# Merges, output projection and up projection of a hybrid layer: splits issued one stage earlier, single-pass loops written out

## The chip, the cores and the metric

The kernel runs on one core of a Trainium2 chip. The metric is device time in microseconds (us). TensorE (PE) multiplies, VectorE (DVE) and ScalarE (ACT) do the elementwise work, SyncE (SP) issues most loads, GpSimd (POOL) a few stores. Every engine runs its own instructions in the order written; engines meet only at semaphores.

## The reference, cut to what matters

Two transformer blocks, sequence 512, width 1024, everything in float32. The change touches the end of the first block:

```
oa = gated delta rule (8 heads);  ob = retention (4 heads)       # before the change's stages
ya = oa @ w_br_a;  yb = ob @ w_br_b                               # 2048 -> 1024 each
mix = (sigmoid(gate_a) * ya + sigmoid(gate_b) * yb) @ w_out       # the gates are 1024 columns each of xn @ w_in
x = x + rmsnorm(mix, norm_mix_post)
hn = rmsnorm(x, norm_mlp_pre)
ff = square(relu(hn @ w_up)) @ w_down                             # 1024 -> 4096 -> 1024
x = x + rmsnorm(ff, norm_mlp_post)
```

The second block (neighbourhood, grouped and memory attention, 16 experts) follows and is not touched.

## The kernel before, in words

A float32 product is made of three passes. Each operand is split in two parts: ACT writes the high part (`high`, L81 to L83), DVE the low part as operand minus high part (`low`, L86 to L88), and PE multiplies low by high, high by high, high by low (`product`, L91 to L96). So each weight piece of 128 x 1024 words costs one `high` on ACT, one `low` on DVE and 24 matmuls of 512 columns on PE. The high parts lie in a ring of four (`hq`), the weights in three slots (`ring_b`, the same memory as `ring`), loaded by SP, 2 MB each; a low part overwrites its weight in place. The activations are transposed, `AT` (low) and `at_hi` (high), 4 row tiles of 128 beside one another.

The stages around the change, in the order in which PE runs them:

- End of head 3 of the retention: PE `scores_b`, `values_b` (fp32 matmuls), ACT the row norms (`attn_b`), DVE `gate_b` (L2353), PE `turn_b` (16 transposes, L1643), DVE `out_b` (L2361).
- Four merges: (x, c) = (0,0), (0,1), (1,0), (1,1), with x the branch and c the half of the columns. Each has 4 gates (24 matmuls each), then 4 blocks b of the branch product (48 matmuls each): 288 matmuls of 512 columns. It needs 12 weight pieces w0 to w11: w0 to w3 for the gates, w4 to w11 for the branch. For c = 0 the branch output `oT` (16 blocks) is loaded from DRAM (`load_o`, L491) and split too, 8 `high` and 8 `low`. The result goes to `mixT` (DVE L2404, or L2406 and L2407).
- Output projection (`tail_major`, L1695): 8 weight pieces and 4 pieces of `mixT` are split; steps n = 0 to 3 run over all four row tiles, then per tile n = 4 to 7. A step (n, t) is 6 matmuls. Between, each tile is normalised twice and turned (`turn_o`, 8 transposes a tile, L1726).
- Up projection (`mlp_up`): 32 groups g of 24 matmuls, relu by DVE (L2498), square by ACT (L1140).
- Down projection: two halves of 16 steps of 24 matmuls, which split the weights and `ffT`.

Each of the later halves (merge c = 1, up projection i = 1) is written as a hardware loop that runs once: `with pe.Fori(1, 2) as c: merge(0, c)`. In the order written, each engine finishes one stage before it begins the next stage's splits: DVE's and ACT's `merge` begins with split w0, after the last product of the merge before; `mixT` is split after the last merge (`act.wait_ge(*m_vec[1]("mix3", 1))`, L1095); the pieces of the second up loop and of the down projection likewise. SP loads `oT` for x = 0 after `b_vec("oT3.3")` and the store `o.3` (L495, L496).

Of the kernel before, what the change touches and what calls it, by code (L numbers as in the profile page):

```python
# [6 lines left out]
ALU = mybir.AluOpType  # L7
# [91 lines left out]
def build(nc, T, out):  # L99
    with ExitStack() as ctx:  # L100
# [85 lines left out]
        (mix_hi,), _ = carve(work, 8192, [(KB, 512)])  # L186
        (ff_hi, ff_lo), _ = carve(work, 0, [(4, 2, 512), (4, 2, 512)])
# [219 lines left out]
        final_banks = (0, 1, 2, 6, 7, 3, 4, 5)  # L407
        l_ring = [ring[1], ring[0]]
# [12 lines left out]
        def only(i):  # L421
            return isinstance(i, int) and i == 0
# [5 lines left out]
        def _(sp):  # L428
# [52 lines left out]
            def load_merge(x, c, before=None):  # L481
# [3 lines left out]
                srcs = (W[:, :, bass.ds(c * 512 + col, 512)], wb[0][:, :, bass.ds(c * 512, 512)], wb[1][:, :, bass.ds(c * 512, 512)])  # L485
                for q in range(3):
                    sp.wait_ge(*(before[q] if before else m_pe[x](("gate3", "lo3", "y3")[q], c - 1)))
                    m_w[x][q].start()
                    m_w[x][q].mark(sp.dma_start(ring_b[q], srcs[q]), "w")
# [4 lines left out]
            load_merge(0, 0, [bg_pe(f"g{g}.3") for g in (3, 7, 11)])  # L494
            sp.wait_ge(*b_vec("oT3.3"))  # L495
            sp.wait_ge(*ob_st_s("o.3"))  # L496
            load_o(0)
            with sp.Fori(1, 2) as c:
                load_merge(0, c)
            load_merge(1, 0, [m_pe[0](n, 1) for n in ("gate3", "lo3", "y3")])  # L500
            load_o(1)
            with sp.Fori(1, 2) as c:
                load_merge(1, c)

            WO = T["w_out"].rearrange("(k p) n -> p k n", p=P)
            for q in range(2):
                sp.wait_ge(*m_pe[1](("gate3", "lo3")[q], 1))
                o_w[q].mark(sp.dma_start(ring_b[q], WO[:, :, q * 512:(q + 1) * 512]), "w")
            sp.wait_ge(*m_vec[1]("mix3", 1))
# [6 lines left out]
            def load_up(i, before=None):  # L516
                for q in range(4):
                    sp.wait_ge(*(u_pe(f"g{4 * q - 5}", i) if q >= 2 else before[q] if before else u_pe(f"g{4 * q + 11}", i - 1)))
                    u_w[q].start()
                    u_w[q].mark(sp.dma_start(ring[q % 2], WU[:, :, bass.ds(i * 2048 + q * 512, 512)]), "w")  # L520
            load_up(0, [m_pe[1]("y3", 1), o_pe("m31")])
            with sp.Fori(1, 2) as i:
                load_up(i)

            def load_down(c):
                for q in range(4):
                    if q >= 2:
                        sp.wait_ge(*d_pe(f"p{4 * q - 5}.{c}"))
                    else:
                        sp.wait_ge(*(d_pe(("p11.0", "m3.0")[q]) if c else u_pe(f"g{4 * q + 11}", 1)))  # L530
                    d_w[q].mark(sp.dma_start(ring[q % 2], WD[q][:, :, c * 512:(c + 1) * 512]), f"w.{c}")
# [274 lines left out]
        def _(act):  # L806
# [228 lines left out]
            attn_b(B_HEADS - 1)  # L1035

            def merge(x, c):


                m_act[x].start()  # L1040
                first = only(c) and c == 0
                for n in range(12):
                    b = n - 4
                    if n % 4 == 0 and n < 8:
                        act.wait_ge(*m_w[x][n // 4]("w", c))
                    if n == 5:
                        act.wait_ge(*m_w[x][2]("w", c))
                    if n < 4:
                        if first and n == 0:
                            act.wait_ge(*(bg_pe("g11.3") if x == 0 else m_pe[0]("y3", 1)))  # L1050
                        elif not first:
                            act.wait_ge(*m_pe[x](("lo2", "y2", "lo3", "y3")[n], c - 1))
                    elif n < 8:
                        act.wait_ge(*m_pe[x](f"gate{b}", c))
                        if not first:
                            act.wait_ge(*m_vec[x](f"mix{b}", c - 1))
                        elif x == 1:
                            act.wait_ge(*m_vec[0](f"mix{b}", 1))
                        elif b == 0:
                            act.wait_ge(*b_vec("PT3.3"))  # L1060
                        m_act[x].mark(act.activation(sg[:, b, :], psum[b % 2][:, :], ACT.Sigmoid), f"sg{b}")
                    else:
                        act.wait_ge(*m_pe[x](("lo0", "y0", "lo1", "y1")[n - 8], c))
                    slot, q = (0, n) if n < 4 else (1 + n % 2, b // 2)
                    high(act, m_act[x], h_col[n % 4], ring_b[slot][:, :, q * P:(q + 1) * P], f"w{n}")
                    if n == 7 and first:
                        act.wait_ge(*ot_ld[x]("o"))
                        for k in range(8):
                            high(act, ot_act[x], oT_hi[:, 2 * k:2 * k + 2, :], oT[:, 2 * k:2 * k + 2, :], f"o{k}")
            merge(0, 0)  # L1070
            with act.Fori(1, 2) as c:
                merge(0, c)
            merge(1, 0)
            with act.Fori(1, 2) as c:
                merge(1, c)
# [19 lines left out]
            act.wait_ge(*m_vec[1]("mix3", 1))  # L1095
            for n in range(8):
                if n % 2 == 0:
                    high(act, o_act, mix_hi[:, n:n + 2, :], mixT[:, n:n + 2, :], f"mix{n // 2}")
                if n < 2:
                    act.wait_ge(*o_w[n]("w"))  # L1100
                if n >= 4:
                    act.wait_ge(*o_pe(f"p{n - 4}"))
                high(act, o_act, h_row[n % 4], ring_b[n % 2][:, n // 2 * 2:n // 2 * 2 + 2, :], f"w{n}")
            def norm_o(t):
                post_norm(o_act, o_vec, lambda t, c: 2 * t + c, lambda t, c: o_pe(f"m{t}{c}"), True, o_hN, t)

            def up_first(n):
                act.wait_ge(*o_pe(("r4", "r5", "m30")[n]))
                high(act, u_act, h_col[n], ring[0][:, :, n * P:(n + 1) * P], f"w{n}")
            u_act.start()  # L1110
            for t in range(3):
                norm_o(t)
            act.wait_ge(*u_w[0]("w"))
            up_first(0)
            split_tile(o_act, o_vec("AT01"), 0)
            norm_o(3)
            split_tile(o_act, o_vec("AT11"), 1)
            split_tile(o_act, o_vec("AT21"), 2)
            up_first(1)
            split_tile(o_act, o_vec("AT31"), 3)  # L1120
            up_first(2)

            def mlp_up(i):
                if not only(i):
                    u_act.start()
                for g in range(0 if only(i) else -3, 16):
                    n = g + 3
                    if n < 16:
                        if n % 4 == 0:
                            act.wait_ge(*u_w[n // 4]("w", i))  # L1130
                        if n >= 4:
                            act.wait_ge(*u_pe(f"g{n - 4}", i))
                        elif not only(i):
                            act.wait_ge(*u_pe(f"g{n + 12}", i - 1))
                        high(act, u_act, h_col[n % 4], ring[n // 4 % 2][:, :, n % 4 * P:(n % 4 + 1) * P], f"w{n}")
                    if g < 0:
                        continue
                    act.wait_ge(*u_vec(f"relu{g}", i))
                    at = bass.ds(i * 16 + g, 1)
                    u_act.mark(act.activation(ffT[:, at, :], ffT[:, at, :], ACT.Square), f"ff{g}")  # L1140
                    if only(i) and 9 <= g < 13:
                        q = g - 9
                        act.wait_ge(*p_vec(f"memT{q}"))
                        high(act, p_act, mem_hi[:, 2 * q:2 * q + 2, :], memT[:, 2 * q:2 * q + 2, :], f"mh{q}")
            mlp_up(0)
            with act.Fori(1, 2) as i:
                mlp_up(i)

            def mlp_down(c):
                for n in range(16):  # L1150
                    if n % 4 == 0:
                        act.wait_ge(*d_w[n // 4](f"w.{c}"))
# [264 lines left out]
        def _(pe):  # L1417
# [270 lines left out]
            with pe.Fori(1, 2) as c:  # L1688
                merge(0, c)
# [1227 lines left out]
```

## Time and profile before

| | us |
|---|---|
| median of 3 runs (2643.02 to 2647.59) | 2643.35 |
| the profiled execution, its own time | 2646.1 |
| its span, first to last instruction | 2644.3 |
| PE busy | 2454.5 (93%) |
| DVE busy | 1111.4 (42%) |
| ACT busy | 834.2 (32%) |
| mean granted TensorE clock, 1.0 is full | 0.970 |

The span and the run's own time differ by 1.8 us, which lies around the instructions. A matmul's duration in a row (0.39 us for 512 columns) includes its pipeline; how fast PE gets on is read from the starts. "[5.36 <-DVE work L2353]" at the end of a row says that the engine was idle 5.36 us before it, and who ended that.

### The profile page before, as it was taken

Reading aid. Unit: us, or ns where it says so; the run is one execution under the profiler, and the core shown is the slowest. Engines: PE = TensorE matmul, PEld = TensorE weight load, DVE = VectorE, ACT = ScalarE, POOL = GpSimd, SP = SyncE. Lnnn points to the kernel's source line nnn. Section 1 sums busy time; section 2 is a strip of 40 time slices with the busy share of each in tenths; the row PEclk is TensorE's granted clock in tenths of the full one; section 3 lists DMA queues with packets and bytes.
Section 4 is the critical chain, followed back from the end, with each engine's and each line's share of the span. In section 5 each row is a group of like instructions: output and inputs, shape, how many; then the busy total and the mean of one; then the engine's idle time right before and its main releaser. Section 6 shows DMA issues by size and latency. Waiting matters only on the chain.

```text
span 2644.3 us, 31184 instructions
## 1 busy us (share of the span) xinstructions
PE 2454.5 (93%) x13320; PEld 1833.8 (69%) x13320; DVE 1111.4 (42%) x1503; ACT 834.2 (32%) x1311; POOL 174.4 (7%) x159
## 2 busy tenths in 40 slices
PE   7999999999998999987999999978899969999997
PEld 5787888877776777776787887855678844454442
DVE  5747566343433323245334454457543441111223
ACT  6444534232322313133224343435522221110101
POOL 0202021111110000000000001121000000000000
PEclk9999999999998999998999999989999989999998
DMA  4112203132223223231222233231222369999995
GB/s 156 64 49 81 96 33 120 65 112 84 100 71 143 103 77 123 96 129 68 82 96 96 96 134 117 90 108 64 80 96 80 145 249 394 428 428 427 427 428 223
DMA packets 116665, 400.43 MB, mean 151 GB/s; under 512 B 6320, under 2 KB 24240, under 8 KB 103600
## 3 DMA queue, kind: packets, MB, share of 16 engines
q1 hardware_dynamic: 112368, 383.76, 37.9%
q0 software_dynamic: 4160, 14.68, 1.6%
q8 instruction: 106, 1.74, 0.3%
q14 instruction: 31, 0.25, 0.0%
HBM read 384.53 MB, written 13.89 MB: 151 GB/s over the span
## 4 chain that ended last, share of the span: by engine, by line
PE 83%; DVE 9%; ACT 4%; issue 2%; DMA 1%; SPq 0%; DVEq 0%; ACTq 0%
PE banks L94 19%; PE banks L96 19%; PE banks L95 19%; PE banks L2060 8%; PE banks L2089 4%; PE banks L2017 2%; DVE ring_split L88 1%; PE banks L1636 1%; PE banks L1534 1%; ACT halves_split L83 1%; DVE work L2791 1%; DMA work<-v_rows 1%; PE banks L1540 1%; DVE const L2585 1%; PE banks L1626 1%
## 5 line engine op out<-in xcount | busy, mean ns | idle before, releaser
L94 PE MATMUL banks<-work_split,ring_split 128*128 128x512 f32 x1536 | 624.7, 407 | 33.0 <-DVE ring_split L88 16.0
L88 DVE TENSOR_TENSOR ring_split<-ring,halves_split 128x1024 fp32r<-128x1024 f32 x284 | 355.8, 1267 | 673.0 <-ACT halves_split L83 672.9
L95 PE MATMUL banks<-work_split,halves_split 128*128 128x512 f32 x1536 | 605.9, 394 | 0.0
L96 PE MATMUL banks<-activations_T_split,halves_split 128*128 128x512 f32 x1184 | 467.6, 395 | 0.0
L83 ACT ACTIVATE halves_split<-ring 128x1024 fp32r<-128x1024 f32 x284 | 295.2, 1053 | 311.2 <-PE banks L96 255.9
L94 PEld LDWEIGHTS banks<-work_split,ring_split 128*128 128x128 f32 x1536 | 293.0, 191 | 106.1 <-issue 25.5
L95 PEld LDWEIGHTS banks<-work_split,halves_split 128*128 128x128 f32 x1536 | 293.6, 191 | 58.8 <-issue 1.0
L96 PE MATMUL banks<-ring_split,work_split 128*128 128x512 f32 (+1 forms) x736 | 285.2, 388 | 0.0
L95 PE MATMUL banks<-halves_split,work_split 128*128 128x512 f32 x672 | 263.9, 393 | 0.0
L96 PEld LDWEIGHTS banks<-activations_T_split,halves_split 128*128 128x128 f32 x1184 | 225.9, 191 | 48.9
L94 PE MATMUL banks<-halves_split,work_split 128*128 128x512 f32 x384 | 152.5, 397 | 10.1 <-DVE work_split L88 5.1
L96 PEld LDWEIGHTS banks<-ring_split,work_split 128*128 128x128 f32 x736 | 139.6, 190 | 28.5
L95 PEld LDWEIGHTS banks<-halves_split,work_split 128*128 128x128 f32 x672 | 127.7, 190 | 26.9 <-issue 0.7
L96 PE MATMUL banks<-work_split,halves_split 128*128 128x512 f32 x352 | 138.1, 392 | 0.0
L94 PE MATMUL banks<-halves_split,activations_T_split 128*128 128x512 f32 x288 | 116.5, 405 | 4.6 <-DVE ring_split L88 4.6
L2060 PE MATMUL banks<-ring,work 128*64 128x512 f32 x384 | 112.2, 592 | 5.6 <-DVE work L2791 5.2
L2060 PE MATMUL banks<-work 128*64 128x512 f32 x384 | 112.2, 593 | 4.2 <-DVE work L2791 4.2
L870 ACT ACTIVATE work<-banks 128x512 f32<-128x512 f32 x60 | 35.9, 598 | 192.4 <-PE banks L96 192.2
L1379 ACT ACTIVATE work<-banks 128x512 f32<-128x512 f32 x16 | 15.8, 1090 | 255.1 <-PE banks L2060 255.1
L2771 DVE TENSOR_TENSOR work<-banks,work 128x512 f32<-128x512 f32 x16 | 11.1, 692 | 202.2 <-ACT work L1379 202.2
L94 PEld LDWEIGHTS banks<-halves_split,work_split 128*128 128x128 f32 x384 | 73.4, 191 | 26.6 <-issue 5.9
L2060 PEld LDWEIGHTS banks<-ring,work 128*64 128x64 f32 x384 | 38.7, 137 | 71.2 <-issue 71.2
(339 smaller groups left out, 3186.4 us busy)
## 6 DMA issues: line engine op xcount, KB each, us to landing
ring<-w_in_in SPq DMA_DIRECT2D x31, 2048.0 KB, 7.8
work<-w_gate_up_in SPq DMA_DIRECT2D x24, 2048.0 KB, 18.2
ring<-w_gate_up_in SPq DMA_DIRECT2D x24, 2048.0 KB, 18.1
ring<-w_down_in SPq DMA_DIRECT2D x20, 2048.0 KB, 10.1
work<-w_down_in SPq DMA_DIRECT2D x9, 2048.0 KB, 14.9
ring<-w_in_in SPq DMA_DIRECT2D x17, 1024.0 KB, 7.7
ring<-w_up_in SPq DMA_DIRECT2D x8, 2048.0 KB, 7.8
halves<-w_gate_up_in SPq DMA_DIRECT2D x8, 2048.0 KB, 19.6
```

The lines of the kernel that those rows point to most:

```text
L83: s.mark(act.activation(R(dst), src, ACT.Copy), what)
L88: s.mark(dve.tensor_tensor(R(dst), src, R(hi).bitcast(F32), ALU.subtract), what)
L94: pe.matmul(out, R(ll), R(rh), start=start, stop=False)
L95: pe.matmul(out, R(lh), R(rh), start=False, stop=False)
L96: return pe.matmul(out, R(lh), R(rl), start=False, stop=stop)
L870: g_act.mark(act.activation(dst, src, func), f"e{i}")
L1534: mm = pe.matmul(bank_c[j][h, c], X[j][h, t, :], PP[j][h, t, :], start=True, stop=True)
L1540: mm = pe.matmul(bank_b[j][h, c], PP[j][h, t, :], X[j][h, t, :], start=True, stop=True)
L1626: mm = pe.matmul(psum[2 + m][:, m * P:], qkT[:, 2 + k, m * P:(m + 1) * P], qkT[:, k, m * P:], start=(k == 0), stop=(k == 1))
L2017: mm = pe.matmul(psum[b // 4][:, b % 4 * P:(b % 4 + 1) * P], XR[:, t, b * P:(b + 1) * P], SP[:, t, :], start=(t == 0), stop=(t == NT - 1))
L2060: mm = pe.matmul(psum[3 + c % 2 * 2 + c // 2][64 * e:64 * e + 64, :], xst[:, 2 * q + k, 64 * e:64 * e + 64], weights(12 * p + 2 * q + e, k ...
L2089: mm = pe.matmul(psum[4 + n][64 * e:64 * e + 64, :], actT[:, 4 * a + k, 64 * e:64 * e + 64], weights(12 * p + 8 + 2 * a + e, k * DM + n * ...
```

## The change

- The single-pass loops are written out; signal names carry the half (`w0.1`), addresses become constants. The number of instructions in the bodies stays.
- PE runs the first two gates of merge (0,0) between `values_b(3)` and `turn_b(3)`. ACT and DVE split w0 to w3 of it before `attn_b(3)` and `gate_b(3)`. DVE's `out_b(3)` moves behind w5. SP loads `oT` of x = 0 after `b_pe("O3.3")`, and the wait for store `o.3` moves to the load for x = 1.
- `oT` is split in groups of three beside the gates 1 to 3, no more after all of them.
- In each merge ACT splits w0 to w3 of the next one at its end; DVE splits w0 in front of product 2, w1 in front of product 3.
- `mixT`'s first two pieces are split in merge (1,1); `mix_hi` moves to `at_hi`'s memory. The order of the output projection's pieces becomes `o_order`, which uses the first column half's slot first. The first three up pieces are split between the output pieces 5 and 7, with buffers of their own (`up_hi`).
- The norms: the gain `norm_mix_post` is multiplied before the root is there, residual add and scale are one instruction, `norm_mlp_pre` is a row (`pre_row`, one more 512 KB load on SP in front of the memory tokens and the first up weights) multiplied in with the second norm, and the transposed tiles are split straight from PSUM in halves. ACT loads the Sqrt table ahead.
- `turn_o(1)` runs inside tile 3; the up projection begins with groups 0 to 2 on the columns 0 to 255 (row tiles 0 and 1), `turn_o(3)` behind group 0, then the columns 256 to 511.
- The first three weight pieces and two `ffT` pieces of the down projection are split in g = 28 to 30; `ffs` has 8 places.

The core of the diff:

```diff
             scores_b(B_HEADS - 1)
             values_b(B_HEADS - 1)
+            gate_m(0, 0, 0)
+            gate_m(0, 0, 1)
             turn_b(B_HEADS - 1)
...
-            with pe.Fori(1, 2) as c:
-                merge(0, c)
+            for m in range(4):
+                x, c = merge_of(m)
+                for b in range(2 if m == 0 else 0, 4):
+                    gate_m(x, c, b)
                 for b in range(4):
+                    branch_m(x, c, b)
...
-            sp.wait_ge(*b_vec("oT3.3"))
+            sp.wait_ge(*b_pe("O3.3"))
+            load_o(0)
+            load_merge(0, 1)
+            load_merge(1, 0)
             sp.wait_ge(*ob_st_s("o.3"))
-            load_o(0)
...
             x_back.mark(sp.dma_start(XR, T["x"].rearrange("(t p) d -> p t d", p=P)), "x")
             o_row.mark(sp.dma_start(row, T["norm_mix_post"].broadcast_to([P, DM])), "row")
+            o_row.mark(sp.dma_start(pre_row, T["norm_mlp_pre"].broadcast_to([P, DM])), "pre")
...
+            # ACT, one merge
+                for b in range(4):
+                    gate_m(x, c, b)
+                    split_m(x, c, b + 4)
+                    if c == 0 and b:
+                        if b == 1:
+                            act.wait_ge(*ot_ld[x]("o"))
+                        for k in range(3 * b - 3, min(3 * b, 8)):
+                            high(act, ot_act[x], oT_hi[:, 2 * k:2 * k + 2, :], oT[:, 2 * k:2 * k + 2, :], f"o{k}")
+                if (x, c) == (1, 1):
+                    high_mix(0)
+                    high_mix(1)
+                for n in range(8, 12):
+                    split_m(x, c, n)
+                if (x, c) != (1, 1):
+                    for n in range(4):
+                        split_m(nx, nc_, n)
...
+            # ACT, output projection
+            high_o(4)
+            high_o(5)
+            high_up(0)
+            high_up(1)
+            high_o(6)
+            high_up(2)
+            high_o(7)
+            act.activation(nmax[:, 0:1], eps, ACT.Sqrt)
...
+            # DVE, norms of the output projection
+            for t in range(2):
+                weighed_o(t)
+                post_o(t)
+                pre_o(t)
+            weighed_o(2)
+            post_o(2)
+            low_t(0)
+            pre_o(2)
+            weighed_o(3)
+            post_o(3)
+            low_t(1)
+            low_t(2)
+            pre_o(3)
+            low_t(3)
...
+            # PE
+            turn_o(2)
+            for t in range(2):
+                pe.wait_ge(*o_vec(f"ATl{t}1"))
+            for g in range(3):
+                pe.wait_ge(*u_vec(f"w{g}"))
+                up(g, 0, 256)
+                if g == 0:
+                    turn_o(3)
+            for t in range(2, 4):
+                pe.wait_ge(*o_vec(f"ATl{t}1"))
+            for g in range(32):
+                if g < 3:
+                    mm = up(g, 256, 512)
...
+                # ACT (DVE the same with low_), behind the square of group g
+                if 28 <= g < 31:
+                    high_down(g - 28, 0)
+                if 28 <= g < 30:
+                    high_ff(g - 28, 0)
```

## Rows read from the trace of the kernel before

**Rows 1.** The page: busy time of each engine, share of the span, instructions.
```profile
PE 2454.5 (93%) x13320; PEld 1833.8 (69%) x13320; DVE 1111.4 (42%) x1503; ACT 834.2 (32%) x1311; POOL 174.4 (7%) x159
```

**Rows 2.** Waits of PE, 834 to 1400 us: total, times, longest.
```profile
PE banks L94 <- DVE ring_split L88: 17.6, 6, 5.0
PE banks L94 <- DVE work_split L88: 13.3, 3, 5.1
PE banks L1726 <- DVE work L2433: 10.2, 2, 8.1
...
PE banks L94 <- DVE activations_T_split L88: 5.1, 1, 5.1
```

**Rows 3.** Stretches: length, busy (count) PE, PEld, DVE, ACT, POOL; PEclk, DMA, GB/s.
```profile
834.40:919.90 85.50, 74.03 (x305) 60.36 (x304) 31.23 (x32) 28.52 (x32) 0.75 (x1) 0.90 0.29 103
919.90:989.00 69.10, 67.20 (x288) 55.10 (x288) 16.93 (x16) 11.49 (x13) 0.00 (x0) 0.98 0.26 92
989.00:1064.40 75.40, 68.82 (x289) 56.16 (x288) 28.18 (x27) 25.10 (x27) 0.00 (x0) 0.95 0.38 139
1064.40:1134.00 69.60, 66.94 (x289) 54.99 (x288) 19.70 (x20) 11.49 (x13) 0.00 (x0) 0.98 0.26 92
1134.00:1206.60 72.60, 52.37 (x224) 42.91 (x224) 42.73 (x57) 32.47 (x53) 0.00 (x0) 0.83 0.32 118
1206.60:1389.90 183.30, 179.56 (x784) 148.02 (x784) 62.48 (x69) 49.16 (x64) 0.00 (x0) 0.98 0.23 81
1389.90:1401.10 11.20, 6.12 (x15) 4.86 (x16) 9.32 (x9) 8.32 (x9) 0.00 (x0) 0.70 0.51 189
```

**Rows 4.** Timeline of PE, 878.90 to 884.81: first and last of 27 starts.
```profile
878.90 0.39 PE L94 MATMUL banks<-work_split,ring_split 128*128 128x512 f32 x1
...
884.81 0.39 PE L96 MATMUL banks<-work_split,halves_split 128*128 128x512 f32 x1
```

**Rows 5.** Timeline of PE at the start of merge (0,0), and one turn at 1180.
```profile
839.83 3.67 PE L1643 MATMUL banks<-const,work 128*128 128x128 f32 x16 [5.36 <-DVE work L2353]
845.48 0.79 PE L94 MATMUL banks<-work_split,ring_split 128*128 128x512 f32 x1 [1.98 <-DVE ring_split L88]
...
1180.02 1.03 PE L1726 MATMUL banks<-const,work 128*128 128x128 f32 x8
```

**Rows 6.** Stretches: half-clock start, long dense stretch, 48 matmuls of 256 columns, a turn.
```profile
840.00:848.00 8.00, 6.03 (x22) 5.14 (x23) 6.71 (x8) 0.59 (x1) 0.75 (x1) 0.50 0.27 101
1402.00:1566.00 164.00, 164.00 (x725) 135.78 (x724) 71.81 (x66) 59.40 (x66) 0.00 (x0) 1.00 0.26 93
1577.60:1583.60 6.00, 6.00 (x51) 5.89 (x50) 6.00 (x8) 2.65 (x4) 0.00 (x0) 1.00 0.90 316
1180.00:1186.40 6.40, 6.40 (x34) 5.35 (x33) 4.19 (x8) 2.90 (x8) 0.00 (x0) 1.00 0.00 0
```

**Rows 7.** Timeline of DVE across a merge boundary; at 1139.75 ACT's splits.
```profile
919.92 0.69 DVE L2404 TENSOR_TENSOR work<-banks,residual 128x512 f32<-128x512 f32 x1 [10.19 <-PE banks L96]
920.53 4.62 DVE L88 TENSOR_TENSOR ring_split<-ring,halves_split 128x1024 fp32r<-128x1024 f32 x4
...
1139.75 1.99 ACT L83 ACTIVATE halves_split<-ring 128x1024 fp32r<-128x1024 f32 x2
```

**Rows 8.** DMA: size and time to landing, in the windows of their issue.
```profile
work<-o_a SPq DMA_DIRECT2D x1, 4096.0 KB, 13.7
work<-o_b SPq DMA_DIRECT2D x1, 4096.0 KB, 18.3
ring<-w_up_in SPq DMA_DIRECT2D x1, 2048.0 KB, 15.9
```

**Rows 9.** Timeline, last tile of the output projection, DVE and ACT.
```profile
1192.21 0.59 ACT L1081 ACTIVATE work<-banks 128x512 f32<-128x512 f32 x1
...
1195.09 1.23 DVE L2427 TENSOR_TENSOR residual<-residual,work 128x1024 f32<-128x1024 f32 x1
1196.34 1.06 ACT L1087 ACTIVATE work<-residual 128x1024 f32<-128x1024 f32 x1 [2.93 <-DVE residual L2427]
```

More of the change, by code:

```diff
@@ L514, in _, with load_up @@
             WD = T["w_down"].rearrange("(a k p) n -> a p k n", p=P, a=4)
[L516 to L523, printed above, removed]
+            def load_up(n):
+                if n >= 2:
+                    sp.wait_ge(*u_pe(f"g{4 * n - 5}"))
+                else:
+                    sp.wait_ge(*(m_pe[1]("y3.1"), o_pe("m31"))[n])
+                u_w[n % 4].mark(sp.dma_start(ring[n % 2], WU[:, :, n * 512:n * 512 + 512]), f"w{n // 4}")
+            for n in range(8):
+                load_up(n)
             def load_down(c):
@@ L1034, in _ @@
                 step_b(h)
-            attn_b(B_HEADS - 1)
[L1037 to L1069, printed above, removed]
@@ L1077, in post_norm, with high_mix @@
+            def high_mix(n):
+                act.wait_ge(*m_vec[1]("mix3.0" if n < 2 else f"mix{2 * n - 3}.1"))
+                high(act, o_act, mix_hi[:, 2 * n:2 * n + 2, :], mixT[:, 2 * n:2 * n + 2, :], f"mix{n}")
+            for n in range(4):
+                split_m(0, 0, n)
+            attn_b(B_HEADS - 1)
+            for m in range(4):
+                merge(*merge_of(m))
             def post_norm(act_s, vec_s, bank, last, prenorm, hN, t):
@@ L1104, in norm_o @@
[L1104 to L1144, printed above, removed]
@@ L1160, in mlp_down @@
[L1160 to L1161 removed]
+                    if c or n >= 3:
+                        high_down(n, c)
+                    if c or n >= 2:
+                        high_ff(n, c)
             for c in range(2):
@@ L1687, in _, with tail_major @@
-            merge(0, 0)
-            with pe.Fori(1, 2) as c:
-                merge(0, c)
-            merge(1, 0)
-            with pe.Fori(1, 2) as c:
-                merge(1, c)
-            def tail_major(vec_s, pe_s, hi, lo, view, rows, between, second=None):
+                    branch_m(x, c, b)
+            def tail_major(vec_s, pe_s, hi, lo, view, rows, order, between, second, inside=None):
                 def step(n, t):
-                    k, c = n // 2 * 2, n % 2
+                    k, c = order[n]
@@ L1704, in tail_major @@
                     pe.wait_ge(*vec_s(f"w{n}"))
-                    if n == 1 and second:
+                    if order[n] == (0, 1):
                         second()
@@ L1757, in _, with up @@
-            mlp_up(0)
-            with pe.Fori(1, 2) as i:
-                mlp_up(i)
+            pe.wait_ge(*m_act[1]("sg3.1"))
+            pe.wait_ge(*m_vec[1]("mix2.1"))
+            tail_major(o_vec, o_pe, mix_hi, mixT, ring_b, h_row, o_order, lambda t: turn_o(0) if t == 2 else None,
+                       lambda: pe.wait_ge(*m_vec[1]("mix3.1")), lambda t, n: turn_o(1) if (t, n) == (3, 5) else None)
+            turn_o(2)
+            def up(g, c0, c1):
+                for k in range(KB):
+                    mm = product(pe, psum[g % 4][:, c0:c1], (up_slot(g)[:, k, :], up_piece(g)[:, k, :]), (at_hi[:, k, c0:c1], AT[:, k, c0:c1]),
+                                 k == 0, k == KB - 1)
+                return mm
@@ L2415, in post_norm @@
+            decay_b(B_HEADS - 1)
+            for n in range(4):
+                split_m(0, 0, n)
+            gate_b(B_HEADS - 1)
+            for m in range(4):
+                merge(*merge_of(m))
             def post_norm(act_s, vec_s, bank, rowsig, pt_tmp, t):
```

475 lines of the change are left out of this document (279 added, 196 removed).

## The prediction

> **What bounds the kernel now.** The page comes first: PE is busy 93% of the span, DVE and ACT under half [rows 1]. So time can only be won where PE stands idle or runs at its lower clock, and the next view is the list of what PE waited for in the part that the change touches. Nearly every wait there ends with DVE, although DVE has time to spare: 17.6 us for low parts of weights, 13.3 for low parts of activations, 10.2 for a normalised tile, 5.1 for the last turned tile [rows 2], and 5.36 before the 16 transposes of head 3, which is the wait that the list's cut leaves out [rows 5]. Together 51.6 us. The reader is to see that these are not waits for a busy engine but for an order: at a merge boundary DVE writes the last product at 919.92 and only then, back to back, the low parts that the next gates need [rows 7].
>
> The third view is the table of stretches, for the idle time has a companion. Between two starts PE takes (884.81 - 878.90) / 26 = 0.227 us for a matmul of 512 columns [rows 4]. A merge has 288, which is 65.5 us; the stretches of the four merges are 85.5, 69.1, 75.4 and 69.6 [rows 3], more than 65.5 plus their waits. The rest is the clock: after 5.36 and 1.98 us of idleness the granted clock is 0.50, that is 1.2 of 2.4 GHz [rows 6], and each matmul issued then costs about 0.2 us more. A dense stretch of 164 us shows 1.00 throughout [rows 6]. So each wait is worth itself and one to three us behind it, and length minus counted work gives both at once; I use that.
>
> No loop overhead shows: the four low parts at 920.53 follow the product without a gap [rows 7], and each loop runs once. Writing the loops out is worth 0 by itself (below and above: 0.1 us a boundary, some 0.5 in all, from the gap at 919.92); what counts is the order that it allows.
>
> **Part by part.** Unit costs: a high part 1.0 us on ACT, a low part 4.62 / 4 = 1.15 on DVE, a 128x512 product from PSUM 0.69 [rows 7]; 8 transposes 1.03 with their pipeline, 0.85 to the next start, at full clock, 16 of them 3.67 at half clock [rows 5].
>
> (a) Merge (0,0). The stretch of 85.5 holds 65.5 of matmuls and 16 transposes, 1.7 at full clock: 18.3 lost. After: the two gates (48 x 0.227 = 10.9 us) run while ACT takes the row norms and DVE gates the head; DVE is done with that at 839.8, PE asks for it only at about 834.4 + 10.9 = 845.3. The load of `oT` is now issued at 834.5 instead of 849.4 and takes 13.7 [rows 8], landing at 848.2, while the first branch product comes at 834.4 + 65.5 / 3 + 1.7 = 857.9. In between DVE has four products for head 3 (4 x 0.81), the first three pieces of `oT` by 854.7, w6, three more by 859.3; PE needs piece k at 857.9 + 1.36 k. The last two, behind w7, are there at 863.0, needed at 866. Nothing late: gain 18.3. If the two gates did not start at once (w0 needs ACT and DVE before 834.4, both idle from 826), the loss would be 1 to 2.
>
> (b) Merge (0,1): 69.1 - 65.5 = 3.6 lost to w0, which now is split before product 2. Its slot is loaded when the gates end, 44 us earlier. Gain 3.6.
>
> (c) Merge (1,0): 75.4 - 65.5 = 9.9. w0 as in (b). `oT` of x = 1 takes 18.3 [rows 8] beside a weight load and is issued no earlier than before, 0.5 after the last product. Count from that product: landing 18.8, gates end 21.8. ACT makes o0 to o2 by 21.7, then the late sigmoid and w6, o3 to o5 by 26.2, w7, o6 and o7 by 29.7; DVE follows by about 1.2 to 1.8: o3 25.7, o5 28.0, o6 30.3, o7 31.5. PE wants them at 25.9, 28.6, 30.0, 31.3. About 0.4 late. Gain 9.5. A load 2 us later would make it 7.5.
>
> (d) Merge (1,1): 69.6 - 65.5 = 4.1, all of it w0. Gain 4.1. The two pieces of `mixT` that ACT and DVE take on in this merge lie in the 16 us between w7 and w8.
>
> (e) Output projection to the first up matmul: 72.6 us with 192 matmuls (43.6) and 32 transposes (3.4), 25.6 lost. Its start waits for nothing any more. Three new costs. First, the up weights: their load took 15.9 from 1136.91, so it landed 18.8 after the last product [rows 8, 3]; with one more 512 KB in front, at about 0.4 MB a us, 20.2. ACT, in order, stands at that load in front of output pieces 6 and 7: up0 21.3, up1 22.3, o6 23.3, up2, o7 25.2, and DVE has o6 at 24.9 and o7 at 27.2. PE wants them at 24.5 and 25.9: about 1.4 late. Second, the tail. Let M be the last output matmul. On the last tile the residual add began 2.88 after its second square [rows 9], of which about 1.4 were the two products by the root; now they stand in front of it, and of the second one (0.69) the root hides half. So the residual begins at M + 2.0 and, 1.23 long, ends at 3.25; then DVE takes the two halves of tile 1 (2 x 0.69), so PE may begin the up projection at M + 4.75 with tiles 0 and 1. `turn_o(2)` fills 0.85 of it; 3.9 idle. DVE goes on with tile 2 to 6.1 and ends `hn3` at M + 7.5; PE has used 3.0 for the half group and asks at 7.75. Tile 3's low halves are there at about 11.1; the half groups 1 and 2 end at 14.6. Third, the half groups: 48 matmuls of 256 columns took 6.0 us [rows 6], 0.125 each; 144 of them cost 18.0 instead of 72 x 0.227 = 16.3, so 1.7 more. Sum 7.0; gain 18.6. The slow matmuls at the start of the up projection stay (they are in (f)). Bounds: 20.2 if the weights are in time and DVE's order hides half of the idleness, 13 if the load crawls at `o_a`'s 0.3 MB a us (landing 22, 3.2 late) and the clock stays low over the half groups.
>
> (f) Up projection: 183.3 with 768 matmuls (174.6) and 16 transposes (1.7), 7.0 lost. 1.6 is the slow start, kept; 5.4 is the wait for piece 16 and its clock, and the pipeline of three pieces ahead now runs through. Gain 5.4.
>
> (g) Down projection: 11.2 us up to full clock for 14 matmuls (3.2): 8.0 lost. The load is issued when g27 ends, as before; w0 is there 7.9 later, 2.4 after g28. ACT has w0 and the first `ffT` piece 4.5 after g28, DVE 5.7, with 16.3 us until the down projection. Pieces 2 and 3 of `ffT` wait for the last group and have 10.9 us. Gain 8.0. What is queued behind the waiting split in g = 28 is relu29 on DVE, needed for bank 1 a whole group later.
>
> Sum: 18.3 + 3.6 + 9.5 + 4.1 + 18.6 + 5.4 + 8.0 = 67.5 us. The profiled execution took 2646.1 (span 2644.3, 1.8 around it), which gives 2578.6; it is 2.75 above the median of the runs, and from 2643.35 the time is 2575.9. I forecast 2576.
>
> The granted clock once more, because the change puts transposes between short groups of matmuls. One turn of 8 inside dense work ran at 0.1 us each with the clock at 1.00, and so did what followed [rows 5, 6]. The Trainium skill, "TensorE: Matmul & The Clock Gate", section "Part 4: PE-mode transpose", states that transposes don't count as PE work for the clock gate in the way matmuls do and don't bring its full rate. By that rule `turn_b` and the turns around the up projection's start would cool the engine; the trace can't refute it, as its one full-speed turn is short and lies in dense work.
>
> **The rivals.**
>
> R1, the clock falls at the turns. 16 transposes between gates would be 3.7 instead of 1.7 and 13 gate matmuls behind them 0.2 dearer (2.0 + 2.6, priced as after the turn at 839.83 [rows 5]); the half groups around `turn_o(3)` would take 0.21 for a matmul over two groups instead of 0.125 (48 x 0.085 = 4.1), less 1.6 counted already. Together 7: 2583. For it: the slow starts follow turns at 845 and 1206. Against it: real idleness stands before each of these.
>
> R2, the waits come back as new ones. ACT and DVE are queues, and a split that now stands in front of a needed product or sigmoid blocks it where its weights or its buffer come late; the up weights are the case that I can see, `oT` of (1,0) the next. If half of (b), (d), (f), (g) and of the tail remained, that is 0.5 x (3.6 + 4.1 + 5.4 + 8.0 + 12) = 16.5, it is 2592. Against it: in all of these the slack worked out is over 5 us.
>
> R3, slower than before. Denser work could make the chip grant less. It decides at a point: PE would have to spend 67.5 / 0.5 = 135 us of the 499 that remain of these 566.7 at 1.2 GHz, and at half of them it would be 2576 + 125 = 2701. Against it: 164 dense us at 1.00 [rows 6].
>
> R4, the change doesn't do what it says: the first product in each stage still finds its split behind another wait, since the order in DVE's queue and not PE's asks decides. Then only the work moved in (a) and (c) pays, some 25 us: 2618.
>
> **How the numbers follow.** The forecast holds with 0.62, R1 0.15, R2 0.15, R4 0.04, R3 0.03; 0.01 is for something without effect. The forecast's own range is 2571 to 2581 (the bounds of (c), (e)). To leave no more than 2 in 10 out, the range takes in R1 and most of R2: 2569 to 2591. What a measurement can tell from no change is 0.2%, 5 us: faster 0.95, same 0.01, slower 0.04.
>
> **What would show it.** In the changed kernel's rows: no wait of PE over 1 us from the end of `values_b` to the output projection's pieces 6 and 7, and the four merges 65 to 66 us each, the first with its transposes; about 1 us before each of those two pieces, on low parts of `ring`; one wait of some 4 us between `turn_o(2)` and the half group 0, with slow matmuls behind it; from there to the second half of the down projection none, where before 3.65 and 5.10 stood. The transposes of `turn_b` at 0.1 us refute R1, at 0.23 they bear it out. I am wrong in mechanism if the sum of PE's waits falls by about 45 us and the time doesn't follow by 60 or more: then something else, after this stage, gave the end.

## The result, and the profile after

The changed kernel takes 2576.41 us (median of 4 runs, 2572.77 to 2577.82) against 2643.86 for the kernel before in the same comparison; the ratio is 0.974, 95% interval 0.9728 to 0.9752. The forecast was 2576, in a range of 2569 to 2591. The profiled execution took 2575.19, with a span of 2573.3.

The waits of PE in the changed stages, 834 to 1330 us of the changed kernel, in the columns of [rows 2]: 51.6 us have become 5.1.

```profile
PE banks L94 <- DVE activations_T_split L88: 3.5, 1, 3.5
PE banks L94 <- DVE work_split L88: 0.8, 2, 0.7
PE banks L94 <- DVE ring_split L88: 0.8, 2, 0.6
```

The same seven stretches as in [rows 3], of the changed kernel (the four merges, output projection to the first up matmul, up projection, first 11 us of the down projection):

```profile
833.30:900.30 67.00, 67.00 (x305) 55.73 (x304) 28.73 (x31) 24.80 (x29) 0.75 (x1) 1.00 0.37 133
900.30:965.60 65.30, 65.30 (x290) 54.08 (x289) 17.14 (x17) 14.69 (x17) 0.00 (x0) 1.00 0.27 97
965.60:1032.60 67.00, 66.04 (x289) 53.80 (x288) 27.96 (x27) 21.99 (x24) 0.00 (x0) 1.00 0.43 157
1032.60:1098.00 65.40, 65.40 (x291) 54.15 (x290) 23.27 (x24) 16.45 (x18) 0.00 (x0) 1.00 0.27 96
1098.00:1148.90 50.90, 46.72 (x216) 38.06 (x214) 30.88 (x43) 26.07 (x50) 0.00 (x0) 1.00 0.43 157
1148.90:1328.40 179.50, 179.46 (x865) 152.27 (x866) 71.07 (x80) 55.95 (x72) 0.00 (x0) 0.99 0.25 88
1328.40:1339.60 11.20, 11.20 (x51) 9.26 (x50) 6.54 (x6) 5.92 (x7) 0.00 (x0) 1.00 0.54 189
```

The reader is to see two columns: PE's busy time now equals the length in four of the seven and misses it by 0.04 us in a fifth (the up projection), and the granted clock, which was 0.70 to 0.98, is 1.00 but for 0.99 in the up projection. The merges are 67.0 (with 16 transposes), 65.3, 67.0 and 65.4 us, where a merge's matmuls are 65.5 by [rows 4].

Next the timeline of PE at the first merge: the turn of head 3 now stands between two gates without idle time, 16 transposes in 1.67 us (843.92 to 845.59), against 5.36 of idleness and 3.67 of transposes in [rows 5].

```profile
843.69 0.39 PE L96 MATMUL banks<-activations_T_split,halves_split 128*128 128x512 f32 x1
843.92 1.91 PE L1701 MATMUL banks<-const,work 128*128 128x128 f32 x16
845.59 0.48 PE L94 MATMUL banks<-work_split,ring_split 128*128 128x512 f32 x1
```

And what PE still waits for: in merge (1,0) for the first branch pieces, in the output projection for pieces 6 and 7, and before the first half group.

```profile
987.96 0.47 PE L94 MATMUL banks<-work_split,ring_split 128*128 128x512 f32 x1 [0.68 <-DVE work_split L88]
996.95 0.50 PE L94 MATMUL banks<-work_split,ring_split 128*128 128x512 f32 x1 [0.16 <-DVE work_split L88]
...
1122.52 0.50 PE L94 MATMUL banks<-halves_split,work_split 128*128 128x512 f32 x1 [0.16 <-DVE ring_split L88]
1124.80 0.50 PE L94 MATMUL banks<-halves_split,work_split 128*128 128x512 f32 x1 [0.60 <-DVE ring_split L88]
...
1148.94 0.43 PE L94 MATMUL banks<-work_split,ring_split 128*128 128x256 f32 x1 [3.46 <-DVE activations_T_split L88]
```

To compare kernels stage by stage I take the starts of the loads that wait for a stage's last product (SP's issues), since they are the same events in every kernel. By them, from the last gemm of head 3 to the product that ends merge (0,0), and on to the load behind the down projection's first half:

| stage | before | after | gained | forecast |
|---|---|---|---|---|
| (a) merge (0,0) with the turn | 98.3 | 80.0 | 18.4 | 18.3 |
| (b) merge (0,1) | 69.1 | 65.3 | 3.8 | 3.6 |
| (c) merge (1,0) | 75.4 | 67.1 | 8.4 | 9.5 |
| (d) merge (1,1), to the residual's load | 71.0 | 66.7 | 4.3 | 4.1 |
| (e), (f) output and up projection | 254.4 | 229.0 | 25.4 | 24.0 |
| (g) down projection, first half | 160.6 | 152.3 | 8.3 | 8.0 |
| sum | 728.8 | 660.4 | 68.5 | 67.5 |

The spans differ by 71.0. Of the 2.5 us outside the stages, 1.3 lie ahead of them and 1.2 behind, where both kernels do the same work. In the 14 profiles of this study the start of the first stage lies anywhere from 819.1 to 822.3, and the part behind the last stage takes 1092.4 to 1096.9 whatever the kernel. Single executions scatter by up to 5 us outside of what is studied here, so a verdict on a few us is read from the stages and not from the total.

Two rows of the table differ between executions too. Row (a) of the old order took 98.3, 97.1, 98.1 and 97.1 us in four executions (the kernel before twice, the one with its loops written out twice). And (e), (f) depend on whether half clock follows the wait of 3.46: where it does not, they are 1.5 us shorter (the section on the late gates shows both cases).

### The profile page after: what moved, and what is told of

Its sections match the earlier page's. It is cut to its first block, busy times and chain, and to the rows that moved or that the text cites. A ratio compares the mean times of both kernels' runs of the same rounds, so it can differ in the third digit from the quotient of the medians.

```text
span 2573.3 us, 31308 instructions
## 1 busy us (share of the span) xinstructions
PE 2428.5 (94%) x13392; PEld 1820.3 (71%) x13392; DVE 1108.2 (43%) x1499; ACT 834.7 (32%) x1316; POOL 174.4 (7%) x159
## 4 chain that ended last, share of the span: by engine, by line
PE 83%; DVE 8%; ACT 4%; DMA 3%; issue 2%; SPq 1%; DVEq 0%; ACTq 0%
PE banks L94 19%; PE banks L96 18%; PE banks L95 18%; PE banks L2128 9%; PE banks L2157 4%; PE banks L2085 2%; PE banks L1694 1%; PE banks L1592 1%; DVE ring_split L88 1%; ACT halves_split L83 1%; DVE work L2896 1%; DMA work<-o_b 1%; PE banks L1598 1%; DMA work<-v_rows 1%; DVE const L2690 1%
## 5 line engine op out<-in xcount | busy, mean ns | idle before, releaser
L94 PE MATMUL banks<-work_split,ring_split 128*128 128x512 f32 (+1 forms) x1560 | 623.5, 400 | 11.3 <-DVE activations_T_split L88 3.5
L95 PE MATMUL banks<-work_split,halves_split 128*128 128x512 f32 x1512 | 591.2, 391 | 0.0
L96 PE MATMUL banks<-activations_T_split,halves_split 128*128 128x512 f32 x1160 | 454.4, 392 | 0.0
L94 PEld LDWEIGHTS banks<-work_split,ring_split 128*128 128x128 f32 x1560 | 295.0, 189 | 80.6 <-issue 12.3
L95 PEld LDWEIGHTS banks<-work_split,halves_split 128*128 128x128 f32 x1512 | 285.3, 189 | 56.8 <-issue 1.2
L96 PEld LDWEIGHTS banks<-activations_T_split,halves_split 128*128 128x128 f32 x1160 | 218.9, 189 | 47.2
L95 PEld LDWEIGHTS banks<-halves_split,work_split 128*128 128x128 f32 x672 | 126.2, 188 | 26.4 <-issue 0.7
L96 PE MATMUL banks<-work_split,halves_split 128*128 128x512 f32 x352 | 137.0, 389 | 0.0
L2128 PEld LDWEIGHTS banks<-ring,work 128*64 128x64 f32 x384 | 38.8, 137 | 71.2 <-issue 71.2
L2128 PEld LDWEIGHTS banks<-work 128*64 128x64 f32 x384 | 38.7, 137 | 69.5 <-issue 69.4
## 6 DMA issues: line engine op xcount, KB each, us to landing
ring<-w_gate_up_in SPq DMA_DIRECT2D x24, 2048.0 KB, 18.4
```

The lines of the kernel that those rows point to most:

```text
L94: pe.matmul(out, R(ll), R(rh), start=start, stop=False)
L95: pe.matmul(out, R(lh), R(rh), start=False, stop=False)
L96: return pe.matmul(out, R(lh), R(rl), start=False, stop=stop)
L2128: mm = pe.matmul(psum[3 + c % 2 * 2 + c // 2][64 * e:64 * e + 64, :], xst[:, 2 * q + k, 64 * e:64 * e + 64], weights(12 * p + 2 * q + e, k ...
```

## The experiments

**Loops alone.** The kernel before, with its loops written out:

```diff
-            with pe.Fori(1, 2) as c:
+            for c in (1,):
                 merge(0, c)
```

(and the same in the eleven other places, on all engines)

> The kernel before with its single-pass loops written out and nothing else. Order theory (the gain is the order of the splits alone): 2643.9, within 0.5 us, all idle times of PE as before (17.6, 13.3, 10.2, 5.4, 5.1). Rival, loop overhead (branches, registers in addresses and waits are part of the 67.5 us): 2 us or more faster, up to 20.

Measured: 2640.87 against 2644.73, ratio 0.9987 (0.9977 to 0.9997). That is neither 0 nor a clear 3 us; the waits of PE are those of before but for 0.7 us more in the turns (10.9 for 10.2), and the stages sum up to 0.4 us less. So it was timed again.

> The kernel before with its loops written out, timed once more, since the first timing gave 0.9987 (0.9977 to 0.9997) and its trace showed only 0.4 us of difference in the stages. Order theory (the loops cost nothing): the ratio lies between 0.9995 and 1.0005. Rival, loop overhead outside what the rows show: 0.9987 again, 3 us.

Measured: 2646.32 against 2644.87, ratio 1.0005 (0.9996 to 1.0014), in its profile the same list of waits:

```profile
PE banks L94 <- DVE ring_split L88: 17.6, 6, 5.0
PE banks L94 <- DVE work_split L88: 13.3, 3, 5.1
PE banks L1726 <- DVE work L2433: 10.9, 2, 9.0
PE banks L1643 <- DVE work L2353: 5.4, 1, 5.4
PE banks L94 <- DVE activations_T_split L88: 5.1, 1, 5.1
```

The first comparison alone excludes a ratio of 1 and the second does not, and the two intervals barely touch: a difference of 0.1% is not settled by one comparison. What holds is that no wait went away, and that writing the loops out gained at most 0.23% (the lower end of the first interval), where the change gained 2.6%. It was the means, not the gain.

**The next merge's gates late.** The changed kernel, with DVE's w0 and w1 behind the last product again:

```diff
                 if m:
+                    for n in range(4):
+                        split_m(x, c, n)
-                    split_m(x, c, 2)
-                    split_m(x, c, 3)
...
                     elif m < 3:
-                        split_m(*merge_of(m + 1), b - 2)
+                        pass
```

> The changed kernel, but DVE makes the low parts w0 and w1 of the next merge only after the merge's last product. Order theory: the three merge boundaries get back 3.8 + 4.3 + 4.2 = 12.3 us (idle 1.9 to 2.6 each and 1.5 to 1.8 of half clock behind it), 2589. Rival, the waits are hidden by work queued elsewhere (ACT still takes its high parts early, so that DVE catches up): under half of it, 2582 or less.

Measured: 2582.15, ratio 0.9766 (0.975 to 0.9782), 5.7 us above the changed kernel and not 12.3: the order theory's figure missed, and the time is the rival's. But not for the rival's reason. The waits did come back; in this kernel's timeline they are, at the three boundaries:

```profile
901.80 0.50 PE L94 MATMUL banks<-work_split,ring_split 128*128 128x512 f32 x1 [1.92 <-DVE ring_split L88]
...
969.29 0.50 PE L94 MATMUL banks<-work_split,ring_split 128*128 128x512 f32 x1 [1.91 <-DVE ring_split L88]
...
1037.51 0.50 PE L94 MATMUL banks<-work_split,ring_split 128*128 128x512 f32 x1 [2.65 <-DVE ring_split L88]
```

The merges are 67.5, 67.5 and 69.7 us long against 65.3, 67.1 and 66.7: 2.2, 0.4 and 3.0 more, together 5.6. Two things make the difference to 12.3. No half clock followed these waits (each was priced with 1.5 to 1.8 us of it). And in merge (1,0) the wait at the start stands in for the later one, since the branch pieces, which were 1.8 us late, now are in time: the two are not additive. Three more executions show what the clock does behind such waits.

> The kernel with the late w0 and w1 once more, for its clock. Its three waits of 1.9, 1.9 and 2.65 us were followed by full clock in the first profile, where the kernel before had half clock behind waits of 1.9, 2.5 and 2.7. Chance theory (whether the clock falls behind a wait of this length changes from execution to execution): at least one of the three merges (0,1), (1,0), (1,1) is 1 to 2 us longer than 67.5, 67.5 and 69.7 (up to the residual's load). Rival, history (what PE did in the 100 us ahead decides, the same in each execution): 67.5, 67.5, 69.7 again within 0.2.

> The same, a third execution. Chance theory: with six more waits at least one followed by half clock. Rival, history: again 67.5, 67.5, 69.7 within 0.2.

> The kernel before, once more, for its clock. Chance theory: at least one of its merges (0,1), (1,0), (1,1) differs by 1 us or more from 69.1, 75.4 and 71.0. Rival, history: 69.1, 75.4, 71.0 within 0.2, as in the kernel with its loops written out (69.1, 75.3, 71.0).

Measured: the three merges took 67.5, 67.5, 71.2 in the second execution and 67.5, 69.1, 69.7 in the third; once the wait of 2.65 and once that of 1.92 was followed by half clock, which the third's timeline shows by matmuls 0.42 apart, where 0.23 stood:

```profile
968.44 0.71 PE L94 MATMUL banks<-work_split,ring_split 128*128 128x512 f32 x1 [1.92 <-DVE ring_split L88]
968.95 0.63 PE L95 MATMUL banks<-work_split,halves_split 128*128 128x512 f32 x1
969.37 0.63 PE L96 MATMUL banks<-activations_T_split,halves_split 128*128 128x512 f32 x1
969.80 0.63 PE L94 MATMUL banks<-work_split,ring_split 128*128 128x512 f32 x1
```

The kernel before gave 69.1, 75.3 and 71.0 again. So the same wait of 1.9 us costs 2.2 us in one execution and 3.8 in the next: in this kernel 2 of 9 such waits fell to half clock. In two executions each of the kernel before and of the one with its loops written out it was 12 of 12. Neither theory holds alone. The clock changes from execution to execution in the new order; in the old order the three merges repeat to 0.2 us, though not merge (0,0), where the wait of 1.98 was followed by 13 or 14 slow matmuls in two executions and by 8 in the other two. What decides stays open.

The same chance lies in the changed kernel itself. Its wait of 3.46 before the first half group stands unchanged in seven of the profiles. In four of them half clock followed (the first row below, of the changed kernel), in three it did not (the second row, of the kernel with late w0 and w1): 29.7 us against 28.2 from the last output matmul to the end of group 3.

```profile
1144.60:1174.30 29.70, 26.24 (x186) 25.07 (x184) 14.19 (x20) 11.03 (x19) 0.00 (x0) 0.94 0.20 72
1150.20:1178.40 28.20, 24.74 (x186) 23.57 (x184) 14.19 (x20) 11.03 (x19) 0.00 (x0) 1.00 0.21 76
```

**The turn in front of the gates.**

```diff
+            turn_b(B_HEADS - 1)
             gate_m(0, 0, 0)
             gate_m(0, 0, 1)
-            turn_b(B_HEADS - 1)
```

> The changed kernel, but PE turns head 3 before the first two gates, as before. Order theory: 5.4 idle, 16 transposes at half clock (3.7 for 1.7) and some 13 gate matmuls at half clock (2.6): 10.0 us, 2586.4. Rival, the transposes cool the clock by themselves in either order: only the idle time differs, 5.4 us, 2581.8.

Measured: 2586.03, ratio 0.9776 (0.976 to 0.9793); merge (0,0) took 88.1 instead of 80.0, 8.2 more. The timeline of PE:

```profile
840.53 3.67 PE L1701 MATMUL banks<-const,work 128*128 128x128 f32 x16 [5.36 <-DVE work L2421]
843.86 0.78 PE L94 MATMUL banks<-work_split,ring_split 128*128 128x512 f32 x1
844.43 0.63 PE L95 MATMUL banks<-work_split,halves_split 128*128 128x512 f32 x1
```

5.36 idle, the 16 transposes in 3.33 us (0.21 each), and only five or so slow matmuls behind them (I had priced 13): 5.4 + 1.7 + 1.1 = 8.2. The rival is out: the transposes are slow behind idleness and fast inside dense work (0.10 each from 843.92 on in the changed kernel).

**The branch pieces late.**

```diff
-                    if c == 0 and b:
+                    if c == 0 and b == 3:
-                        for k in range(3 * b - 3, min(3 * b, 8)):
+                        for k in range(8):
```

(on ACT, and on DVE the same behind w7)

> The changed kernel, but the 8 pieces of the branch output are split behind w7, after the last gate, in merges (0,0) and (1,0). Order theory: 3.8 idle and 1.9 of half clock in (0,0), 4.1 and 1.6 in (1,0), where 1.2 is lost now already: 10.2 us, 2586.6. Rival, the load's landing decides and not the order: nothing in (1,0), where the load lands late, so 5.7 us or less in all, 2582.

Measured: 2590.94, ratio 0.9797 (0.9781 to 0.9813); merge (0,0) 85.7, 5.8 more, merge (1,0) 71.1, 4.1 more, together 9.8 of the 10.2 expected. Each has a wait of 4.12 on the low branch pieces and 6 slow matmuls. The rival is out: (1,0) pays too. The total does not fit as well. By the profiles the kernel is 11.9 us longer: 9.8, 0.7 ahead of the stages and 2.8 behind them, less 1.4 because no half clock followed the wait of 3.46 here. By the medians it is 14.5, and what the other 2.6 are no profile shows.

**The up projection begun on four tiles.**

```diff
+            turn_o(3)
-            for t in range(2):
+            for t in range(4):
                 pe.wait_ge(*o_vec(f"ATl{t}1"))
-            for g in range(3):
-                pe.wait_ge(*u_vec(f"w{g}"))
-                up(g, 0, 256)
-                if g == 0:
-                    turn_o(3)
```

> The changed kernel, but the up projection begins on all four row tiles (no half groups, the last turn in front). Counted from the last output matmul M: the last turn runs at M + 7.5 to 9.4 at half clock, its low parts are there at about M + 11.7; now the first half group starts at M + 4.65, and it pays 0.8 for the turn and 1.0 for 144 matmuls of half the width. Order theory: 11.7 - 4.65 - 0.8 - 1.0 = 5.2 us more, 2581.6. Rival, the half groups only move the wait (the weight loads of 128 columns bound them): 2 us or less, 2578.

Measured: 2583.89, ratio 0.9776 (0.9761 to 0.9791). From the last output matmul to the end of group 3 it takes 35.3 us instead of 29.7, 5.6 more (against 28.2, where the changed kernel's tail keeps its clock, it would be 7.1). PE waits 6.01 us for the last normalised tile, turns it at half clock, waits 1.62 for its low part, and begins slowly:

```profile
1152.27 1.97 PE L1786 MATMUL banks<-const,work 128*128 128x128 f32 x8 [6.01 <-DVE work L2559]
...
1155.85 0.76 PE L94 MATMUL banks<-work_split,ring_split 128*128 128x512 f32 x1 [1.62 <-DVE activations_T_split L88]
```

**The down projection's splits late.**

```diff
-                if 28 <= g < 31:
-                    high_down(g - 28, 0)
-                if 28 <= g < 30:
-                    high_ff(g - 28, 0)
```

(and DVE's likewise; all pieces then in `mlp_down`)

> The changed kernel, but the down projection's first pieces are split only after the last up group. Order theory: 5.1 idle and 2.9 of half clock come back, less nothing: 8.0 us, 2584.4. Rival, the weights' load decides: with the loads unchanged nothing comes back, 2576.4.

Measured: 2582.62, ratio 0.9768 (0.9753 to 0.9783); the first step group of the down projection took 28.4 us instead of 21.8, 6.7 more: a wait of 4.78, and 7 or 8 slow matmuls where the kernel before had 14. The mechanism is the order theory's; the clock's share was 1.7 and not 2.9.

**The tail reordered.** What is left before the first half group is a wait for tile 1's low part, which DVE makes behind tile 3's residual:

```profile
1144.07 0.68 DVE L2556 TENSOR_TENSOR work<-banks,work 128x512 f32<-128x512 f32 x1
1145.36 0.16 DVE L2552 TENSOR_TENSOR const<-const 128x1 f32<-128x1 f32 x1 [0.61 <-ACT work L1156]
...
1146.35 1.28 DVE L2562 SCALAR_TENSOR_TENSOR residual<-work,const,residual 128x1024 f32<-128x1024 f32 x1
1147.56 2.48 DVE L88 TENSOR_TENSOR activations_T_split<-banks,work_split 128x512 fp32r<-128x512 f32 x4
```

```diff
             pre_o(2)
+            low_t(1)
             weighed_o(3)
             post_o(3)
-            low_t(1)
             low_t(2)
...
-                if g == 0:
+                if g == 1:
                     turn_o(3)
```

(and `high_t(1)` on ACT in front of `post_o(3)`)

> The changed kernel, with tile 1 split on ACT and DVE in front of tile 3's norm and the last turn behind half group 1. Order theory: the idle 3.46 before the first half group and the half clock behind it (16 matmuls of 256 columns at 0.213 for 0.119, 1.5) go; tile 3's norm moves back by 0.7, under cover of the half groups: 5.0 us less, 2571.4. Rival, the wait moves behind the half groups (the last tile's low parts late for the second halves, as its chain of 11 us is what bounds): 0 to 1 us, 2576.

Measured: 2572.91, ratio 0.9733 (0.9719 to 0.9746). The stretch from the last output matmul to the end of group 3, which took 29.70 in the changed kernel's profile:

```profile
1144.80:1169.50 24.70, 24.70 (x186) 23.55 (x185) 14.15 (x21) 10.16 (x17) 0.00 (x0) 1.00 0.24 86
```

5.0 us less, with no wait behind the half groups. 3.5 of it are idleness that is gone in every execution; the other 1.5 are the half clock, which the changed kernel pays in some executions only (28.2 against 29.7 above), and the expectation counted it whole. The total moved by 3.5, which the scatter would allow either way.

**All orders.** The same, with three loads moved:

```diff
+            sp.wait_ge(*m_pe[1]("y3.1"))
+            u_w[0].mark(sp.dma_start(ring[0], WU[:, :, 0:512]), "w0")
             sp.wait_ge(*m_vec[1]("mix3.1"))
             x_back.mark(...)
...
+                    if (x, c, q) == (1, 0, 2):
+                        ot_ld[1].mark(sp.dma_start(oT[:, 0:8, :], ...[0:8]), "o")
...
-            load_o(1)
+            ot_ld[1].mark(sp.dma_start(oT[:, 8:16, :], ...[8:16]), "p")
```

> The same tail, and three loads moved: the first up weights are issued right after the last product (before the residual, the two rows and the memory tokens), and the branch output of x = 1 comes as two loads of 2 MB, the first in front of the weights. Order theory: 5.0 from the tail, 0.8 from the output pieces 6 and 7, 1.1 from merge (1,0): 6.9 us less, 2569.5. Rival, the DMA queue's total decides (what is put in front pushes back what follows: the residual, or the branch weights w5): 2571.4 or more.

Measured: 2570.51, ratio 0.9721 (0.9708 to 0.9734), against 0.974 for the changed kernel: the fastest of the study, 5.9 us below it by the medians of two separate comparisons, though the two intervals still overlap a little. The stages show it more sharply: merges (0,1) and (1,0) together 130.6 instead of 132.4, which is the 1.8 of the branch pieces, the output projection 45.4 instead of 46.8, the tail 24.7 instead of 29.7, 8.1 us in all (6.9 expected; 1.5 of the 8.1 is the half clock of the changed kernel's profile). From 830 to 1330 us no wait of PE is listed. Merge (1,0), the output projection and the tail:

```profile
966.00:1030.90 64.90, 64.90 (x289) 53.73 (x287) 27.53 (x28) 21.79 (x25) 0.00 (x0) 1.00 0.45 160
1096.10:1141.50 45.40, 45.40 (x211) 37.72 (x210) 27.47 (x36) 23.06 (x43) 0.00 (x0) 1.00 0.40 153
1141.50:1166.20 24.70, 24.70 (x185) 23.54 (x184) 14.16 (x20) 10.16 (x17) 0.00 (x0) 1.00 0.25 86
```

The up weights landed 9.2 us after their issue instead of 16.5. What was pushed back landed later, the residual 12.9 us after its issue instead of 7.8 and the branch weights 14.8 instead of 8.0, but PE waited for none of it: the rival is out in the stages.

## Why the prediction was right, point by point

- The reading of the idle time held. The waits were an order and not a load: DVE's busy time is the same after as before (1108.2 and 1111.4 us), and each part that was undone by itself brought its own wait back (5.4 for the turn, 4.1 twice for the branch pieces, 1.9, 1.9 and 2.65 for the gates, 4.8 for the down projection, 6.0 and 1.6 for the tail). The stages lengthened by 8.2, 9.8, 5.6, 5.6 and 6.7 us, 35.9 of the 68.5. Not undone were the early splits of w0 to w3 in front of head 3, those of `mixT`, the new order of the output pieces, the rewritten norms and the deeper pipeline in front of piece 16 of the up projection. For these the waits of 1.98, 4.99, 10.2 in the turns and 3.65 are gone from the list; how much each part brought is argued from that and not shown.
- (a), (b), (d), (g) came within 0.3 us of their terms. That is less of a feat than it looks: the terms are length minus work in the profile of before, and the gains in the table are taken from the same profile, so that they agree as soon as nothing is left to wait for in the stage. Against the other executions of the old order (a) would have gained 17.1 instead of 18.4.
- The step "each wait is worth itself and one to three us behind it" does not hold in general. Undone singly, the turn brought back 8.2 where 10.0 was expected, (g) 6.7 for 8.0, and the three waits for gates 5.6 for 12.3: in that execution none of them cost more than 0.35 beyond itself.
- (c) was 1.1 us too high. The lateness of the branch pieces was worked out as 0.4 and measured as 1.8, since the load landed 19.5 after its issue and not 18.3, and PE stopped three times, at 987.96, 992.41 and 996.95. By the starts of the matmuls the stops cost 0.91, 0.39 and 0.43. A row's idle time (0.68, none, 0.16) shows less: it counts from the end of a duration of 0.39, while the next matmul would have started after 0.227, and the matmul behind a stop takes 0.1 more. I had worked the queue of ACT and DVE forward with exact meetings and gave the restarts no price.
- (e) and (f) gained 25.4 for 24.0, and would have gained 26.9 without half clock behind the wait of 3.46. Pieces 6 and 7 (idle 0.16 and 0.60 in their rows) cost 1.3 by the starts of the matmuls, where 1.4 was worked out; ACT began the up weights 19.9 after the last product (20.2 in the working). PE's start on the half groups was M + 4.5 (4.75), idle 3.46 (3.9), where M is 1144.4. A matmul of 256 columns took 0.12 and not 0.125, so that the half groups cost 1.0 and not 1.7.
- The one addition that could speak against the change, 512 KB in front of the up weights, cost 1.1 us, where 1.4 was worked out: the up weights were issued 0.5 later behind the last product and took 16.5 to landing for 15.9.
- R1 is refuted here: 16 transposes at 0.10 each with the clock at 1.00 before, in and behind them. The Trainium skill, "TensorE: Matmul & The Clock Gate", section "Part 4: PE-mode transpose", has the transposes not counting for the full rate; this trace shows no cost of it where they take 1.7 us between dense matmuls, and can't tell more. R2 came true only as (c)'s 1.8 us; the 1.3 at pieces 6 and 7 was in the sum already. R3: PE was granted full clock through 138 us in one stretch (846 to 984) and the mean rose from 0.970 to 0.984. R4 is refuted by the list of waits.
- Of the signs named, PE's waits fell by 46.5 us and the time by 67, and the first, second and fourth merge are as said. Merge (1,0) is not: 67.0 where 65 to 66 was named. And the forecast's own range was added up wrongly: the bounds of (c) and (e) give 2574 to 2584, not 2571 to 2581. The measured time lies in both.

The total hit the forecast to 0.4 us, which is partly luck: its terms were off by 1.1 us one way and 1.4 the other, and the four timed executions of the changed kernel lie between 2572.77 and 2577.82.

## What to carry to other kernels

When the fullest engine waits for an engine that is half idle, look at what stands in front of the awaited instruction in that engine's queue: taking the next stage's first operand splits in front of this stage's last products, with a tail arranged the same way, was worth 68 us here with nearly the same instructions (DVE 1499 for 1503, PE 13392 for 13320). Price such a stage as its length minus its counted work at full rate, since the slow clock behind a wait is in it, but don't take that price for the same wait in another kernel. Two waits close behind one another are not additive: removing one may only lengthen the other.

## What the runs showed of the hardware that was not expected

- The clock behind a wait is not a fixed price. Behind waits of 1.9 to 2.7 us half clock (6 to 8 matmuls at 0.43) followed in 2 of 9 cases in three executions of one kernel, and in 12 of 12 in four executions with the old order. Behind the same wait of 3.46 it followed in 4 of 7 executions. Behind the waits of 3.65 to 5.10 at weight and branch pieces it followed in every profile that has them, for 6 to 14 matmuls, which cost 1.5 to 3.0 us. What decides is not shown.
- The clock need not fall at the wait. Behind 1.92 us in the kernel before, five matmuls first run at the full pace, then seven at half:

```profile
921.80 0.50 PE L94 MATMUL banks<-work_split,ring_split 128*128 128x512 f32 x1 [1.92 <-DVE ring_split L88]
...
923.36 0.63 PE L94 MATMUL banks<-work_split,ring_split 128*128 128x512 f32 x1
923.78 0.63 PE L95 MATMUL banks<-work_split,halves_split 128*128 128x512 f32 x1
```

- A stop of PE that a row shows as 0.16 us idle costs 0.4 in all: the matmul that had to wait starts 0.55 after its forerunner (996.95 in the changed kernel) and the next one 0.34 after it, where 0.227 is the pace.
- A matmul of 256 columns runs at 0.12 us in dense work, little over half of the 0.227 of 512, although its weights are 128 columns as well: halving the moving side costs 6% here.
